# Down products in token chunks of 512, 512 and 64, the 64 with their high and low parts side by side

## What is computed

```python
h = rms_norm(x, lw['norm_g'][2]) * (1 + sc_f) + sh_f
f = (jax.nn.silu(h @ lw['w_gate']) * (h @ lw['w_up'])) @ lw['w_down']
x = x + gt_f * rms_norm(f, lw['norm_g'][3])
```

## Time and profile before

| | us |
|---|---|
| time, median of 2 runs | 1936.96 |
| the two runs | 1935.83 and 1938.1 |
| span of the profiled execution (first to last instruction) | 1930.4 |
| PE busy with products in it | 1816.3 (94%) |
| DVE busy | 989.9 (51%) |
| ACT busy | 629.2 (33%) |

### The profile page before, as it was taken

The page is one execution under the profiler, slowest core; times in us unless marked ns, Lnnn a source line. Parts: engine busy times, 40 slices in busy tenths (PEclk is TensorE's granted clock), DMA queues, the critical chain, the costliest instruction groups (busy, mean ns, idle before and its releaser), DMA issues. The chain is left out here.

```text
span 1930.4 us, 41344 instructions
## 1 busy us (share of the span) xinstructions
PE 1816.3 (94%) x17762; PEld 1533.5 (79%) x17762; DVE 989.9 (51%) x1526; ACT 629.2 (33%) x1262; POOL 349.6 (18%) x411
## 2 busy tenths in 40 slices
PE   5999999988998998998899989999999999999996
PEld 3988889566576576666644689999999999999994
DVE  4697765745554654565527643333333333333347
ACT  4744433444444444444423432112112112112114
POOL 0032220235534434444500010000000000000002
PEclk9999999999999998999999999999999999999998
DMA  9367774210110110103132121011011011011122
GB/s 343 122 173 195 186 194 150 64 38 27 51 41 27 51 41 27 51 27 87 53 123 85 63 97 55 23 55 55 22 55 55 23 55 55 22 55 55 44 93 93
DMA packets 126323, 151.19 MB, mean 78 GB/s; under 512 B 83168, under 2 KB 98144, under 8 KB 125824
## 3 DMA queue, kind: packets, MB, share of 16 engines
q1 hardware_dynamic: 126144, 148.56, 24.0%
HBM read 118.05 MB, written 30.50 MB: 77 GB/s over the span
## 5 line engine op out<-in xcount | busy, mean ns | idle before, releaser
L429 PE MATMUL ps<-fhi,whi 128*128 128x364 f32 (+1 forms) x1056 | 349.0, 330 | 7.8 <-DVE wlo L421 5.7
L429 PE MATMUL ps<-flo,whi 128*128 128x364 f32 (+1 forms) x1056 | 346.8, 328 | 0.0
L429 PE MATMUL ps<-fhi,wlo 128*128 128x364 f32 (+1 forms) x1056 | 345.8, 327 | 0.0
L421 DVE TENSOR_TENSOR wlo<-wraw,whi 128x1024 fp32r<-128x1024 f32 x70 | 86.9, 1243 | 244.4 <-ACT whi L417 244.4
L429 PEld LDWEIGHTS ps<-fhi,whi 128*128 128x128 f32 x1056 | 198.5, 188 | 9.5 <-issue 4.4
L429 PEld LDWEIGHTS ps<-fhi,wlo 128*128 128x128 f32 x1056 | 199.2, 189 | 0.0
L429 PEld LDWEIGHTS ps<-flo,whi 128*128 128x128 f32 x1056 | 198.5, 188 | 0.2
L1895 DVE TENSOR_TENSOR acc<-acc,ps 128x364 f32<-128x364 f32 (+1 forms) x240 | 126.6, 531 | 100.8 <-PE ps L2424 100.5
L841 POOL TENSOR_TENSOR nlev<-gm,con 64x256 f32<-64x256 f32 x204 | 152.8, 749 | 114.2 <-DVE gm L1623 100.1
L429 PE MATMUL ps<-hhi,whi 128*128 128x364 f32 (+1 forms) x464 | 161.3, 348 | 1.5 <-DVE hlo L1491 1.2
L2424 PE MATMUL ps<-ahi,dhi 128*128 128x364 f32 (+1 forms) x480 | 158.5, 330 | 2.4 <-DVE acc L1895 2.4
(11 more groups left out here) (249 smaller groups left out, 3357.7 us busy)
## 6 DMA issues: line engine op xcount, KB each, us to landing
wraw<-in_w_tiles SPq DMA_DIRECT2D x68, 512.0 KB, 4.1
late<-in_ada_t SPq DMA_DIRECT2D x32, 512.0 KB, 3.5
ci<-scan SPq DMA_DIRECT2D x17, 768.0 KB, 4.5
draw<-in_w_down SPq DMA_DIRECT2D x20, 512.0 KB, 3.3
slab<-in_ada_w SPq DMA_DIRECT2D x4, 2048.0 KB, 18.0
x<-in_x_t SPq DMA_DIRECT2D x4, 1456.0 KB, 9.6
bg<-bg SPq DMA_DIRECT2D x17, 256.0 KB, 2.8
x<-x_mid SPq DMA_DIRECT2D x1, 4352.0 KB, 12.8
```

The source lines that it names most:

```text
L421: nc.vector.tensor_tensor(wlo[u][:, :, :], wraw[u][:, :, :], whi[u][:, :, :].bitcast(F32), ALU.subtract).then_inc(w_lo, 1)
L429: mm = nc.tensor.matmul(ps[:, 3 * u + c, 0:n], w[u][:, k, :], x[:, k, :], start=(k == 0 and i == 0), stop=(k == KD - 1 and i == 2))
```

## The change

It defines a second list of chunks, DOWN_CH, for the down products of groups 0 to 9: 512 prompt tokens, 512 prompt tokens, and the 64 sample tokens. CH stays in use everywhere else. The unit of the 64 tokens issues four products in the place of six: for each half u, the high weights against the high and the low part of the 64 tokens side by side (128 columns of PSUM, the first 64 for the high part, the next 64 for the low part), and then the low weights against the high part, added to the first 64 columns. DVE adds both column ranges to `acc`, one after the other, the first with a wait for its own end. The high and the low parts now lie in one tensor (`act0`, `act2`), at the same addresses as before, so that one access pattern can reach both. The order of the units, the two banks and the waits stay.

```diff
+DOWN_CH = [(0, 512), (512, 512), (TP, TS)]
...
-        ahi0, alo0, acc, ahi2, alo2, draw, dhi0, dhi1, dlo0, dlo1, sil0, sil1, sil2, end = place(
-            R2, ("ahi0", [P, 2, T], F32R), ("alo0", [P, 2, T], F32R), ("acc", [P, KD, T]), ("ahi2", [P, 2, T], F32R), ("alo2", [P, 2, T], F32R),
+        act0, acc, act2, draw, dhi0, dhi1, dlo0, dlo1, sil0, sil1, sil2, end = place(
+            R2, ("act0", [P, 2, 2, T], F32R), ("acc", [P, KD, T]), ("act2", [P, 2, 2, T], F32R),
...
-        ahi, alo = {0: ahi0, 2: ahi2}, {0: alo0, 2: alo2}
+        both_parts = {0: act0, 2: act2}
+        ahi, alo = ({slot: x[:, part, :, :] for slot, x in both_parts.items()} for part in range(2))
...
             def add_down(g, x):
 
-                k, (a, n) = x // 3, CH[x % 3]
+                k, (a, n) = x // 3, DOWN_CH[x % 3]
                 dve.wait_ge(down_ready, 24 * g + x + 1 + 1)
                 if x == 0:
                     dve.wait_ge(d_added, 24 * g + 1)
+                if n == TS:
+                    step.done(nc.vector.tensor_tensor(acc[:, k, a:a + n], acc[:, k, a:a + n], ps[:, 6 + x % 2, n:2 * n], ALU.add))
                 nc.vector.tensor_tensor(acc[:, k, a:a + n], acc[:, k, a:a + n], ps[:, 6 + x % 2, 0:n], ALU.add).then_inc(d_added, 1)
...
                 for x in range(24):
-                    k, (a, n) = x // 3, CH[x % 3]
+                    k, (a, n) = x // 3, DOWN_CH[x % 3]
                     if not (first and x < 2):
                         pe.wait_ge(d_added, 24 * g + x - 1 + 1)
+                    if n == TS:
+                        for u in range(2):
+                            nc.tensor.matmul(ps[:, 6 + x % 2, 0:2 * n].rearrange("p (a b) -> p a b", a=2), dhi[u][:, P * k:P * k + P],
+                                             both_parts[slot][:, :, u, a:a + n], start=(u == 0), stop=False, skip_group_check=True)
+                            mm = nc.tensor.matmul(ps[:, 6 + x % 2, 0:n], dlo[u][:, P * k:P * k + P], ahi[slot][:, u, a:a + n],
+                                                  start=False, stop=(u == 1), skip_group_check=True)
+                        mm.then_inc(down_ready, 1)
+                        continue
                     for u in range(2):
                         for w, y in ((dhi, ahi), (dhi, alo), (dlo, ahi)):
```

## The result

| | before | after |
|---|---|---|
| time, median of 2 runs, us | 1936.96 | 1987.76 (1986.66 to 1988.86) |
| span of the profiled execution, us | 1930.4 | 1987.1 |
| PE busy, us | 1816.3 | 1846.6 |
| DVE busy, us | 989.9 | 1003.2 |

The kernel became slower: the ratio is 1.0278, with a 95% interval from 1.0246 to 1.0311, or +50.8 us. The forecast was 1990 us. The profiled execution of the changed kernel is the one of 1988.86 us, so 1.8 us of its time lie outside the span.

A forecast was written before the change was run, and what follows sets the result against it. PE alone was taken to bound the mixer. Nine down products at +5.36 us (29.7 for 24.35) and the last at +5.0 gave +53 us: span 1983.7, plus 6.6 to the median, 1990 us; range 1974 to 2004.

The forecast's parts named there:

- The wait at A': A', next tile's first unit, waits for DVE's add of B (second unit, same bank): 0.61 us at seven of eight tiles.
- C no longer covers the add of B: C, the 64-column unit between, shrinks from 1.00 to 0.44 us; the add of B, 512 columns, grows 532 to 686 ns.
- The wide product: Down product: each 512-column product on PE takes 228.6 ns, 213.3 by columns plus 15.3 fixed; bounds 213.3 and 234.9.
- The narrow unit: The 64-token unit's four products each cost about a full weight load, 109 ns, 0.436 us for the unit.
- The upper bound: Narrow unit at the plain float32 rate, four cycles a column: 0.70 us.
- split of unit 8: DVE's 1.22 us weight split behind unit 8's add; PE's old break there, 0.47 us per group, goes.
- B': Next tile's second unit; in the last down product it waits some 0.2 us, a split preceding the narrow unit's adds.
- the stated range: Kernel time 1974 to 2000 us for the wait as forecast (chance 0.86), 1974 to 2004 with half of rival 4.
- Rival 2: Down product: wait hidden, only open weight loads count; +1.08 us each, +10 in all, 1947 us; chance 0.05.
- rival 3: Down product: narrow unit's loads hidden, no wait shows; -0.64 us each, 1930 us; chance 0.02.
- rival 4: Narrow unit takes over 1.05 us and sets the tile's period; at 1.3 us, +8 us each, 2017 us; chance 0.06.
- rival 5: Wide product costs less than its columns, 131 ns; down product -3.3 us each, 1904 us; chance 0.01.

The follow-up runs named there:

- Experiment 1: Changed kernel with a third PSUM bank (5) for the down units: 1949.37 us, 1.0067 to the kernel before.
- 2: Changed kernel, two banks, with the 64-token unit in its old form of six 64-column products and one add: 1986.91 us, 1.0275 to the kernel before.
- 5: Changed kernel with DVE adding the second 512-column unit in two instructions of 256 columns: 1992.44 us, 1.0296 to the kernel before.
- experiment 3: Changed kernel with both a third bank and six narrow products of 64 columns with one add: 1965.81 us, 1.0165 to the kernel before.
- 8: Kernel before, chunks of 364, 364 and 360, with only the third bank added for its down units: 1929.33 us, 0.9967 to the kernel before.
- experiment 7: Changed kernel with the 16 wide units first, then the 8 narrow ones, and a third bank: 1955.73 us, 1.0090 to the kernel before.

## Why the prediction was right

- **The wait at A'.** Forecast 3.79 us per tile, seven waits per down product; measured 3.78 and seven. The chain was right term by term: add started 0.03 behind B's end (0.04 forecast), 0.688 us long (0.686), load 0.05 behind it (0.05). Experiment 1 shows it by taking it away, 2 and 5 by changing one side of it at a time. The step of the prediction that carried most of the forecast, that C no longer covers the add of B, is thus shown and not only its size.
- **The wide product.** Forecast 0.2286 us by 512 / 2.4 and 15.3 ns fixed. Where no wait or narrow unit is near, it takes 0.227, which is 13.4 ns fixed. Behind a narrow unit some take up to 0.236; I have no cause for that. The Trainium skill ("TensorE: Matmul & The Clock Gate", section "Back-to-back issue gap") gives 0.2158 us for an isolated product, the rule weighed in the prediction. These products take more.
- **The narrow unit.** Forecast 0.436 us. In the last tile of a down product it stands without a wait:

```profile
1307.70 0.22 PE L2428 MATMUL ps<-act,dhi 128*128 128x128 f32 x1
...
1308.06 0.41 PE L431 MATMUL ps<-fhi,whi 128*128 128x364 f32 x1
1308.15 0.19 PEld L431 LDWEIGHTS ps<-flo,whi 128*128 128x128 f32 x1
1308.31 0.33 PE L431 MATMUL ps<-flo,whi 128*128 128x364 f32 x1
```

  The projection behind it has a record of 0.41 in place of 0.33, so in effect it starts at 1308.14: 0.44 us. The upper bound (four cycles a column) was not needed; experiment 3 gives 0.113 us for 64 columns.
- **What the change saves.** Six wide products fewer were to save 92 ns a tile, less than four open loads cost. Experiments 1 and 8 agree: without any wait the down product is 25.6 us with the changed chunks and 23.9 with the old ones.
- **The break that goes, and the one that comes.** The wait behind the split of unit 8 has gone. In the last down product there is one wait more, the 71st, at B' behind the split of unit 4; its tile has 3.19 us in the chain where others have 3.01, the 0.2 forecast.
- **The sum.** Forecast 9 x 5.36 + 5.0 = +53 us. Measured: nine cycles that are 5.33 us longer (77.60 against 72.27) and a last down product that is some 4.9 longer, together +53. The 48.00 us of the projections against 47.91 are no slower projections: from the start of the second product to that of the last it is 47.59 us in both kernels (1308.31 to 1355.90, and 1293.89 to 1341.48 before). The 0.09 lies at the end of the narrow unit: the first two products of the projections are recorded 0.25 us apart there (1308.06 and 1308.31) and 0.16 apart before, because the first one in effect starts only at 1308.14. So it belongs to the down product, which is 29.7 us, as forecast. The medians say +50.8 us. The two profiled spans are 56.7 us apart, because the second execution reached its first down product 3.8 us later, in stages that the change does not touch: the chain's entry is at 1201.03 and was at 1197.26, and ahead of it the page after shows a lowered clock in three slices and the one before in one.
- **Luck.** That the total came within 2.3 us of 1990 is partly luck: the executions of the kernel before that ran beside the experiments lie between 1928.87 and 1940.11 us, and both medians are of two runs. The price of a down product, 29.7 us, is not luck. At its low end the stated range does not follow from its own terms: +39 us with nothing fixed, and 6 less for a shorter add, give 1970 us and not 1974.
- **The rivals.** Rival 2 (only the loads) and rival 3 (neither) fall with the 71 waits, rival 4 with the unit of 0.44 us, rival 5 with the product of 0.227. But rival 2's mechanism, weight loads in the open, is what experiment 1 leaves over: 25.6 us, where rival 2 had 25.4.

## What to carry to other kernels

With two banks in turn, the add of one unit has to fit into the one unit that lies between it and the next user of its bank; so look at the shortest unit and its longest neighbour, not at the total of columns or the number of instructions. Chunks of unequal size need either a third bank or a short unit that still covers the longest add. And a product of few columns costs as much as its full weight load here (0.11 us), so the small remainder was cheaper spread over the other chunks than as a unit of its own: 23.9 against 25.6 us per down product, both without a wait.

## What the runs showed of the hardware

- A stretch of 32 narrow products without a gap in PE's records was followed by a fall of the granted clock from 2.4 to 1.2 GHz (0.55 in the mean over 3.2 us), in seven of ten cycles. With waits among them it was ten of ten and cost 1.5 to 2.6 us per cycle, which took back nearly all that the better order had gained. The same products one unit at a time between wide ones left the clock at 1.00. Each of these is one profiled execution.
- An F32R product with a full weight load of its own takes 0.11 us with 64 columns (0.113, experiment 3) and with 128 (0.44 us for the two of each in unit C).
- 512-column products take 0.227 us in a steady run (21.80 us for 96, experiment 7), and 0.224 to 0.236 behind a narrow unit: for some ten products in every tile of experiment 1, but for three at most in six of the eight tiles of the changed kernel's second down product. What makes the difference was not tried.
